# A hybrid attention block on one core: the first 45 microseconds in another order

## What is computed

```
u = RMSNorm(x) ; [qA,kA,vA,qB,kB,vB] = u @ W_in
oA = sliding-window GQA with sinks and T5 bias
oB = differential attention with T5 bias, block-causal mask
h = x + concat(oA, oB) @ W_out
h = h + W_down(relu(RMSNorm(h) @ W_up)^2)
h = h + sigmoid(RMSNorm(h) @ W_gate) * (p @ W_ple)
y = RMSNorm_final(h)
```

## Time and profile before

| | us |
|---|---|
| three executions | 1216.58, 1216.71, 1216.93; median 1216.71 |
| the profiled execution | 1215.57 |
| its span | 1213.7 |
| mean granted TensorE clock in it | 0.996 |
| TensorE busy | 1191.8 (98%) |
| VectorE / ScalarE / GpSimd busy | 710.8 / 518.6 / 600.2 |
| start of the first product | 20.99 |
| start of the broadcast of the roots | 43.09 |

### The profile page before, as it was taken

One profiled execution on the slowest core, in us unless ns is written; L12 is line 12 of the kernel. 1 busy time (PEld: TensorE's weight loads), 2 busy tenths in 40 slices (PEclk: granted clock), 3 DMA queues, 4 the chain that ended last, 5 costly groups with the idle time before them and its releaser, 6 DMA issues.

```text
span 1213.7 us, 14773 instructions
## 1 busy us (share of the span) xinstructions
PE 1191.8 (98%) x5825; PEld 964.1 (79%) x5825; DVE 710.8 (59%) x927; ACT 518.6 (43%) x858; POOL 600.2 (49%) x284
## 2 busy tenths in 40 slices
PE   6999999999999999999999999999999999999997
PEld 5787787877677788888888888888888888888886
DVE  5245556566767457783937829478294692544233
ACT  6435445455655554423424243243342433442223
POOL 3323222232425567655565556655466555565542
PEclk8999999999999999999999999999999999999999
DMA  6811011123612333425234252342523423121203
GB/s 220 282 36 35 18 36 30 40 53 70 191 36 73 101 125 150 177 70 199 95 122 139 70 183 100 134 139 70 176 102 127 151 70 139 52 78 55 58 1 139
DMA packets 104123, 125.75 MB, mean 104 GB/s; under 512 B 21801, under 2 KB 87382, under 8 KB 98678
## 3 DMA queue, kind: packets, MB, share of 16 engines
q1 hardware_dynamic: 103814, 124.18, 31.2%
q10 hardware_dynamic: 240, 0.62, 0.1%
HBM read 111.14 MB, written 16.01 MB: 105 GB/s over the span
## 4 chain that ended last, share of the span: by engine, by line
PE 94%; DVE 3%; ACT 2%; DMA 1%; SPq 0%; issue 0%; DVEq 0%; ACTq 0%
PE ps L1811 51%; PE ps L1495 23%; PE ps L1471 8%; PE ps L1606 3%; PE ps L1629 3%; PE ps L1617 1%; PE ps L1693 1%; PE ps L1679 1%; PE ps L1666 1%; DMA x_raw<-in_x 1%; ACT e_a L1099 1%; PE ps L1538 1%; PE ps L1554 0%; PE ps L1509 0%; PE ps L1799 0%
## 5 line engine op out<-in xcount | busy, mean ns | idle before, releaser
L883 POOL TENSOR_TENSOR w_lo<-w_raw,w_hi 128x1024 fp32r<-128x1024 f32 x57 | 137.9, 2419 | 148.0 <-ACT w_hi L1008 146.9
L1811 PE MATMUL ps<-block_lo,w_hi 128*128 128x512 f32 x472 | 181.1, 389 | 0.0
L1495 PE MATMUL ps<-u_hi,w_hi 128*128 128x512 f32 x416 | 176.3, 424 | 3.8 <-DVE o_bt L2090 1.7
L752 POOL TENSOR_TENSOR w_lo<-w_raw,w_hi 128x1024 fp32r<-128x1024 f32 x38 | 96.1, 2529 | 163.9 <-ACT w_hi L1023 163.9
L1811 PE MATMUL ps<-up_hi,w_hi 128*128 128x512 f32 x448 | 174.9, 390 | 0.0
L1811 PE MATMUL ps<-up_hi,w_lo 128*128 128x512 f32 x448 | 174.3, 389 | 0.0
L1811 PE MATMUL ps<-up_lo,w_hi 128*128 128x512 f32 x448 | 174.3, 389 | 0.0
L1811 PE MATMUL ps<-block_hi,w_hi 128*128 128x512 f32 x440 | 172.0, 391 | 0.0
L1811 PE MATMUL ps<-block_hi,w_lo 128*128 128x512 f32 x440 | 171.3, 389 | 0.0
L1495 PE MATMUL ps<-u_hi,w_lo 128*128 128x512 f32 x416 | 163.4, 393 | 0.0
L1495 PE MATMUL ps<-u_lo,w_hi 128*128 128x512 f32 x416 | 162.8, 391 | 0.0
(11 more groups left out here) (224 smaller groups left out, 2091.8 us busy)
## 6 DMA issues: line engine op xcount, KB each, us to landing
up_lo<-lo_save SPq DMA_DIRECT2D x36, 1024.0 KB, 5.5
w_raw<-in_w_in SPq DMA_DIRECT2D x48, 256.0 KB
w_raw<-in_w_down SPq DMA_DIRECT2D x18, 512.0 KB
w_raw<-in_w_up SPq DMA_DIRECT2D x16, 512.0 KB
raw_x<-in_w_up SPq DMA_DIRECT2D x15, 512.0 KB
raw_x<-in_w_down SPq DMA_DIRECT2D x14, 512.0 KB
x_raw<-in_x SPq DMA_DIRECT2D x8, 512.0 KB, 7.3
h_save<-x_t SPq DMA_DIRECT2D x1, 4096.0 KB, 12.8
```

The source lines that it names most:

```text
L752: nc.gpsimd.tensor_tensor(w_lo[:, s * D:(s + 1) * D], w_raw[:, s * D:(s + 1) * D], w_hi[:, s * D:(s + 1) * D].bitcast(F32), ALU.subtract). ...
L883: nc.gpsimd.tensor_tensor(w_lo[:, s * D:(s + 1) * D], raw, w_hi[:, s * D:(s + 1) * D].bitcast(F32), ALU.subtract).then_inc(lo_done, 1)
L1495: mm = nc.tensor.matmul(bank(bank_), w, xx[:, x0], start=(first and n == 0), stop=(last and n == 2))
L1811: mm = nc.tensor.matmul(o, w, xx, start=(first and m == 0), stop=(last and m == 2), skip_group_check=onto)
```

## The change

- SP: the five loads of the norm vectors are gone from its queue; ScalarE issues them, ahead of its two bias loads. V0 is loaded behind tile 3 and K0 behind tile 4 (before: 2 and 3).
- A third buffer for the gained tiles, `temp_x2`, in the place of `diag`, used by tiles 2 and 6. VectorE's `diagonals(1)` therefore waits for `x_lo` 4. The gain of tile 2 waits for nothing but its transpose.
- The bias matmuls go to banks 5 and 7, behind the copies of tiles 0 and 1, and stand ahead of tile 4's transpose, which waits for `ln_sb` 1; tile 5's waits for `ln_sb` 2.
- TensorE: tile 0 ahead of the g transpose; tile 5 between the two parts of V0's first half, tile 6 behind them, tile 7 in the middle of K0's first half.
- ScalarE: another order of casts and copies; the squares of tiles 1 to 7 all behind the last copy.
- VectorE: another order, written out; the copies of the bias lines ahead of the rest of tile 3.

```diff
+        temp_x2 = at("temp_x2", [P, T], F32, a_rstd)
+        def temp_x(t):
+            return (temp[0], temp[1], temp_x2, temp[1])[t % 4]
...
             for t in range(TT):
                 sp.dma_start(x_raw[:, t * D:(t + 1) * D], x[0, t * P:(t + 1) * P, :]).then_inc(x_in[t], 16)
-                if t == 0:
-
-                    for i, g in enumerate((attn_norm_g[0], mlp_norm_g[0], ple_norm_g[0], final_norm_g)):
-                        sp.dma_start(g_rows[8 * i:8 * i + 8, :], g.rearrange("(j q) -> j q", q=P)).then_inc(g_in, 16)
-                    sp.dma_start(g_rows[32:33, :], subln_g[0].rearrange("(j q) -> j q", j=1)).then_inc(g_in, 16)
-                if t == 2:
+                if t == 3:
                     load_v(0)
-                if t == 3:
+                if t == 4:
                     load_k(0)
...
+            for i, g in enumerate((attn_norm_g[0], mlp_norm_g[0], ple_norm_g[0], final_norm_g)):
+                act.dma_start(g_rows[8 * i:8 * i + 8, :], g.rearrange("(j q) -> j q", q=P)).then_inc(g_in, 16)
+            act.dma_start(g_rows[32:33, :], subln_g[0].rearrange("(j q) -> j q", j=1)).then_inc(g_in, 16)
...
-            for t in range(6):
+            turn_x(0)
+            pe.wait_ge(g_in, 80)
+            nc.tensor.transpose(ps[:, 7 * 512:7 * 512 + 33], g_rows[0:33, :], ident[0:33, 0:33]).then_inc(g_tr, 1)
+            for t in range(1, 4):
                 turn_x(t)
             pe.wait_ge(hot_in, 32)
             for i in range(2):
-                pe.wait_ge(x_h, 3 + i)
-                nc.tensor.matmul(ps[0:12, (1 + 2 * i) * 512:(1 + 2 * i) * 512 + LINE], relb[:, :],
+                pe.wait_ge(x_h, 1 + i)
+                nc.tensor.matmul(ps[0:12, (5 + 2 * i) * 512:(5 + 2 * i) * 512 + LINE], relb[:, :],
                                  hot[:, i * LINE:(i + 1) * LINE], start=True, stop=True).then_inc(ln_ps, 1)
+            turn_x(4)
...
             half_block(0, 0, range(0, 4))
+            turn_x(5)
+            half_block(0, 0, range(4, 8))
             turn_x(6)
-            half_block(0, 0, range(4, 8))
-            turn_x(7)
             pe.wait_ge(lo_done, 2)
             pe.wait_ge(x_h, 4)
-            half_block(1, 0, range(0, 8))
+            half_block(1, 0, range(0, 4))
+            turn_x(7)
+            half_block(1, 0, range(4, 8))
             pe.wait_ge(x_lo, TT // 2)
             pe.wait_ge(x_lo_v, TT // 2)
-            pe.wait_ge(ln_sb, 2)
             half_block(0, 1, range(DT)).then_inc(blk_done, 1)
...
+            def gain_x(t):
+                dve.wait_ge(x_tr, t + 1)
+                if t % 2 and t >= 3:
+                    dve.wait_ge(x_lo_v, t // 2)
+                elif t >= 4:
+                    dve.wait_ge(x_lo, t // 2 - 1)
...
+            gain_x(0)
+            gain_x(1)
+            gain_x(2)
+            rest_x(1)
+            gain_x(3)
+            for i in range(2):
+                dve.wait_ge(ln_ps, i + 1)
+                nc.vector.tensor_copy(lines[:, i * LINE:(i + 1) * LINE],
+                                      ps[0:12, (5 + 2 * i) * 512:(5 + 2 * i) * 512 + LINE]).then_inc(ln_sb, 1)
+            rest_x(3)
+            early_lo(0)
+            gain_x(4)
+            early_lo(1)
+            gain_x(5)
+            gain_x(6)
+            rest_x(5)
+            gain_x(7)
...
+            rest_x(7)
```

More of the change, by code:

```diff
@@ L763, in _ @@
                 pool.wait_ge(x_hi, t + 1)
[L764 removed]
+                nc.gpsimd.tensor_tensor(u_tokens(u_lo, t), temp_x(t)[:, :].rearrange("p (j t) -> p j t", t=P),
                                         u_tokens(u_hi, t).bitcast(F32), ALU.subtract).then_inc(x_lo, 1)
@@ L1032, in gain_hi @@
                 act.wait_ge(x_g, t + 1)
-                nc.scalar.copy(u_tokens(u_hi, t), temp[t % 2][:, :].rearrange("p (j t) -> p j t", t=P)).then_inc(x_hi, 1)
+                nc.scalar.copy(u_tokens(u_hi, t), temp_x(t)[:, :].rearrange("p (j t) -> p j t", t=P)).then_inc(x_hi, 1)
             def square_x(t):
@@ L1041, in square_x, with keep_x @@
                                      accum_out=ssq[:, t:t + 1]).then_inc(x_ss, 1)
+            for i, g in enumerate((attn_norm_g[0], mlp_norm_g[0], ple_norm_g[0], final_norm_g)):
+                act.dma_start(g_rows[8 * i:8 * i + 8, :], g.rearrange("(j q) -> j q", q=P)).then_inc(g_in, 16)
+            act.dma_start(g_rows[32:33, :], subln_g[0].rearrange("(j q) -> j q", j=1)).then_inc(g_in, 16)
             act.dma_start(relb[:, :], rel_bias).then_inc(hot_in, 16)
             act.dma_start(hot[:, :], onehot.rearrange("b c l -> b (c l)")).then_inc(hot_in, 16)
-            square_x(0)
-            for t in range(TT):
-                gain_hi(t)
+            def keep_x(t):
                 nc.scalar.copy(x_t[:, :].rearrange("p (j t) -> p j t", t=T)[:, :, t * P:(t + 1) * P],
                                x_banks(t).rearrange("p (j t) -> p j t", t=P)).then_inc(x_h, 1)
[L1051 to L1054, removed]
+            square_x(0)
+            gain_hi(0)
+            gain_hi(1)
+            keep_x(0)
+            gain_hi(2)
+            keep_x(1)
+            gain_hi(3)
+            early_hi(0)
+            keep_x(2)
+            keep_x(3)
+            gain_hi(4)
+            early_hi(1)
+            keep_x(4)
+            for t in range(5, TT):
+                gain_hi(t)
+                keep_x(t)
+            for n in range(1, TT):
+                square_x(n)
             act.wait_ge(lam_p, 1)
@@ L1542, in _ @@
             pe.wait_ge(const_ok, 3)
-            pe.wait_ge(g_in, 80)
-            nc.tensor.transpose(ps[:, 7 * 512:7 * 512 + 33], g_rows[0:33, :], ident[0:33, 0:33]).then_inc(g_tr, 1)
             def turn_x(t):
@@ L1550, in turn_x @@
                     pe.wait_ge(x_h, t - 3 if t < 6 else t - 1)
+                if 4 <= t < 6:
+                    pe.wait_ge(ln_sb, t - 3)
                 if t == 1:
@@ new lines, in gain_x @@
+            def gain_x(t):
[4 more added lines that the diff above has]
+                    dve.wait_ge(x_lo, t // 2 - 1)
+                nc.vector.tensor_tensor(temp_x(t)[:, :].rearrange("p (j t) -> p j t", t=P),
+                                        x_banks(t).rearrange("p (j t) -> p j t", t=P),
+                                        g_col[:, 0:DT].unsqueeze(2).to_broadcast([P, DT, P]),
+                                        ALU.mult).then_inc(x_g, 1)
@@ new lines, in rest_x, with early_lo @@
+            def rest_x(t):
+                dve.wait_ge(x_hi, t + 1)
+                nc.vector.tensor_tensor(u_tokens(u_lo, t), temp_x(t)[:, :].rearrange("p (j t) -> p j t", t=P),
+                                        u_tokens(u_hi, t).bitcast(F32), ALU.subtract).then_inc(x_lo_v, 1)
+            def early_lo(b):
+                w = slice(b * D, (b + 1) * D)
+                dve.wait_ge(hi_done, b + 1)
+                nc.vector.tensor_tensor(w_lo[:, w], w_raw[:, w], w_hi[:, w].bitcast(F32),
+                                        ALU.subtract).then_inc(lo_done, 1)
@@ new lines, in _ @@
+            rest_x(5)
+            gain_x(7)
+            dve.wait_ge(misc_in, 8 * 16)
+            l4 = lam_in[:, :].rearrange("p (a b d) -> p a b d", b=2, d=HD)
+            nc.vector.tensor_tensor(l4[:, :, 0, :], l4[:, :, 0, :], l4[:, :, 1, :], ALU.mult).then_inc(vch, 1)
+            nc.vector.tensor_scalar(nsink[:, :], sink[:, :], -1.0, None, ALU.mult).then_inc(vch, 1)
+            dve.wait_ge(vch, 3)
+            nc.vector.tensor_reduce(lam_s[:, :], l4[:, :, 0, :], AX_X, ALU.add).then_inc(lam_p, 1)
@@ L2070, in _ @@
             mean_square(1, ssq[:, :])
+            dve.wait_ge(x_lo, TT // 2)
             diagonals(1)
```

32 lines of the change are left out of this document (removed).

## The result

| | before | after |
|---|---|---|
| median of four executions (before: those shown above and one more) | 1216.64 | 1225.18 (1224.31 to 1225.81) |
| ratio, 95% interval | | 1.0070 [1.0053, 1.0088] |
| the profiled execution, its span | 1215.57, 1213.7 | 1224.67, 1222.9 |
| mean granted clock | 0.996 | 0.993 |

What follows compares the result with a forecast made beforehand. TensorE, busy 98% of the span, was taken to bound the kernel. +3.05 up to the broadcast (one low-clock stretch included) and +1.85 for the clock there made +4.9, from 1216.71 to 1221.6, range 1217.4 to 1223.5.

Steps and rivals of the forecast that it cites:

- from the last square's end at 36.64 to the end of `diag` at 39.83: 3.2: Head, behind the squares: mean, power and diagonals take 3.2 us up to the end of `diag`.
- the sum of 15.1: Head, from the end of tile 7's transposes to `diag`: 15.1 us, range 14.6 to 15.6, so the broadcast starts at 46.15.
- 4 us to spare: Q0's weights, cast on ScalarE behind the squares: they and the roots have 4 us of slack, so cost nothing.
- taking the 1.64 of its row: VectorE's line at the start: V0's rest begins at 16.8, takes 1.64 and opens the first product at 18.4.
- land about 5.4: Norm vectors on ScalarE's queue: landing about 5.4, covered by turning tile 0 until 6.6; uncovered lateness is added one for one.
- 1.85 each: Low clock behind the start and at the broadcast: half pace for 3.7 us, +1.85 each, bounds 0 and 3.4.
- Rivals 1 and 2: Head's clock: only one low stretch comes, +3.05, 1219.8, chance 0.21; neither comes, +1.2, 1217.9, chance 0.12.
- the lead at the start is gone by tile 7: Transposes behind the start: first product 2.6 earlier, but three tiles turned behind it, so tile 7's end is +0.9.
- the wait ahead of V0's second half: TensorE waits about 1.1 there for tile 7's rest, in the place of the 0.87 of before.
- `diag` near 46: Sign in the profile after: `diag` near 46, with TensorE idle 3 us ahead of the broadcast, released by it.
- Rival 3: The start decides, not the squares: first product before 17.1 at high clock, at its bound -0.2, 1216.5; chance 0.08.
- Rival 4: A load is late: V0 past 15.5 delays ScalarE's cast and all behind it, +6.4, 1223.1; chance 0.09.

Runs made afterwards that it cites:

- e3: The changed kernel with the five norm-vector loads back on SP's queue behind tile 0: 1224.96, ratio 1.0064.
- e4: The kernel before with only the squares of tiles 1 to 7 moved behind the last copy: 1223.19, ratio 1.0053.
- e2: The changed kernel with one more wait, GpSimd beginning the rest of Q0's weights only behind `diag`: 1221.88, ratio 1.0041.
- e1: The changed kernel with the squares of tiles 1 to 7 back between the tiles, where they stood before: 1219.48, ratio 1.0020.
- e5: The changed kernel with the squares laid into ScalarE's idle times and tile 7's transposes two steps earlier: 1216.46, ratio 1.0000.
- e10: e5 with `block_lo` ahead of a sum in the first MLP chunk, only the attention norm's vector loaded first, second bias copy behind V0's rest: 1214.85, ratio 0.9982.
- e8: The kernel before with squares 1 and 2 behind tile 4's copy, 3 behind 5's, 4 behind 6's, 5 to 7 behind 7's: 1216.86, ratio 0.9998.
- e11: e10 with two filling matmuls in TensorE's waits, the squares placed anew and the lambda sums behind tile 7's rest: 1212.73, ratio 0.9968.
- e6: e5 with matmuls of unused result behind the first bias matmul (one) and tile 4's transposes (two): 1218.19, ratio 1.0006.

## Why the prediction was right in direction and wrong in size

**The step that failed: "from the last square's end at 36.64 to the end of `diag` at 39.83: 3.2", and with it the sum of 15.1.** Measured, it took 5.3 (44.20 to 49.53), since `diag` stood 2.06 behind GpSimd. The stretch from tile 7's transposes to the broadcast took 17.3 (32.26 to 49.58), outside the 14.6 to 15.6 that I gave it, "as every duration has its row". The row of 1.23 was for a `diag` beside an idle GpSimd. I had followed what the squares delay on ScalarE and found that Q0's cast has slack; I did not ask what else starts when they end. The cast comes out right behind them (44.20), its rest is GpSimd's next instruction behind the root, and GpSimd starts it the moment the root is done (46.10), while `diag`, which waits for the same root on another engine, comes 0.14 later. In each run where the cast was done by then, `diag` was second: after, e3 (46.44 and 46.58) and e4 (43.82 and 43.89). Shown by e2, where the broadcast starts 2.07 earlier and the time is 3.3 less, and by e4, where it appears with the squares' place alone. In the forecast's words Q0's weights had "4 us to spare"; what was late was right, but the harm was in their being ready too soon.

A sign lay open in the earlier trace rows: V0's rest with 1.64 among rows of 1.21 to 1.23. I carried it as that operation's duration ("taking the 1.64 of its row"). It was the tail of the same stand: GpSimd's `u_lo` ended at 17.54 there, and the row at 18.62, 1.08 later. GpSimd's row in before:

```profile
15.16 2.38 POOL L764 TENSOR_TENSOR u_lo<-temp,u_hi 128x1024 fp32r<-128x1024 f32 x1 [2.49 <-ACT u_hi L1033]
```

The Trainium skill (SBUF — State Buffer, section "SBUF: two separate sides") has the rule: VectorE with two SBUF inputs and GpSimd share a port pair, whoever starts first holds it for the whole instruction, the other blocks. The trace agrees on both sides, with 3.29 for VectorE behind and 3.04 for GpSimd behind (2.41 alone). With GpSimd's rows of 2.3 to 2.4 it would have given this term a price before the run, and I weighed another page.

**The norm vectors.** By the forecast they "land about 5.4", covered by the turn of tile 0 until 6.6: they landed at 7.47, 5.1 behind their issue, where before's took 3.1. TensorE stood 1.04, and gain 0 came at 8.16 and not 7.4, V0's rest at 17.84 and not 16.8. That it took 1.22 and not 1.64 gave 0.4 back, which is luck, as the 1.64 was misread; 0.25 from its end to the product came on top, and the start came at 19.31 and not 18.4: +0.9, mostly what the forecast's own clause said ("one for one"). That the landing is late because four tiles of x stand on the other queue is argued, not shown: e3 changed queue and place at once, and there the vectors were there by 6.78.

**The low clock, twice.** Both stretches came, as forecast at 0.50. Their size was a little under: behind the start to tile 7's transposes 12.95 instead of the 10.8 at full clock, 2.15; from the broadcast to `q_b` 17.97 instead of before's 15.57, 2.4. I had 1.85 each; together 0.85 short. Rivals 1 and 2 (one stretch or none) are out. The forecast let it fall in the two waits, as in before. That holds for the second; the first time it fell near 16.8, ahead of the wait and while tile 4's transposes ran, as in e1 (16.4) and e5 (15.8); in e3 (14.3), e2 (17.3) and e10 (16.3) it fell in a wait. The rule of the Trainium skill that I weighed (TensorE: Matmul & The Clock Gate, Part 4: PE-mode transpose) changed nothing in the sum. Where the rows bear on it they speak against it: in e8 the clock rose to 1.00 near 18.0, when TensorE had done nothing but transposes since 15.04, and in before near 18.9, behind transposes since 15.19.

**Right as forecast**: the lead at the start is gone by tile 7 (e5: with the squares mended, time as before); the wait ahead of V0's second half (0.99 for 1.1); seven squares in a row (35.59 to 44.2); the order of its causes, with the broadcast late for `diag`. "`diag` near 46" is not among them, though its row begins at 46.24: by the sum it was to be done at 46.15 and thus to start near 44.9. Rival 3, that the start decides, wanted a start before 17.1 at the high clock, which did not come; e11, with a start at 17.76 and the squares placed otherwise, shows what the high clock is worth there (2.36). Rival 4 did not come; V0 was not late.

**The sum, corrected**: 4.9, plus 0.9 for the vectors, 2.1 for the collision and 0.85 for the clock is 8.75, against 8.89 in the head. **Open**: what decides in which short wait the clock falls (e3 and after differ by 2.4 in that, e8 by a second fall), and 0.6 of e2's gain by medians.

## What to carry to other kernels

When work is moved to the end of an engine's queue, look not only at what it makes late but at what it releases all at once when it ends, and on which engines that meets. A row with an odd duration (1.64 among 1.22) can hold a wait inside the instruction: look at the other engine before it is used as a price. And a start won ahead of a wait was worth little here while the clock fell around that wait (e10 against e5: 1.13 at the start, 0.43 at the broadcast); fill it, or win both.

## What the runs showed that I had not expected

- **A busy VectorE row can be a wait.** Behind a GpSimd instruction the VectorE instructions on SBUF operands above show as busy until GpSimd's end and for their own work behind it: 3.29, 3.35 and 3.42 instead of 1.22, which end 1.1 behind GpSimd, and 2.36 instead of 0.16 for `nsink`, which ends with it. VectorE's gains, with one operand in PSUM, don't stand: in after tile 2's took 1.23 from 11.88, in the midst of GpSimd's `u_lo` (10.54 to 12.92).
- **It can make one kernel's runs fall in two groups.** In e5 and e6 a load landed 0.9 to 1.3 later than in before and GpSimd was ahead of `block_lo`, 490 us into the program, for 3 us of the whole (e6: 1214.95 to 1215.69 and 1218.13 to 1218.63).
- **Two or three useless matmuls held the clock at 1.00** through waits in which it fell without them (e6, e11). Their rows take 3.0 in e6 and 2.1 in e11; the first product came 0.16 later than in e5 and at the same 17.76 as in e10.
